# A two-block model on one core: group norms by products with a tile of ones, and the narrow rows of the recurrences made inside the delta projection

## The chip, the cores and the metric

One NeuronCore of a Trainium2 chip. The metric is the device time of the whole program in microseconds, median of three runs. Lower is better.

## The reference, cut to what matters

512 tokens of width 1024 go through a first block (band attention and a state space beside each other, attention to a memory of 256 rows, an expert layer) and twice through a hybrid layer: a gated delta rule (gdn), latent attention (mla) and a state-space duality (ssd) on the same normalised input, gated, added and projected, then a feed-forward part. The change touches normalisations of groups of channels and the small rows that steer both recurrences:

```python
def rmsnorm(x, g):
    return x * lax.rsqrt(jnp.mean(x * x, axis=-1, keepdims=True) + EPS) * g

# in the delta mixer; the duality's dt is made in the same way
beta = jax.nn.sigmoid(b_raw)
g = -jnp.exp(a_log) * jax.nn.softplus(a_raw + dt_bias)
o = gated_delta_chunked(q, k, v, g, beta)        # begins with a cumsum of g over each chunk
o = rmsnorm(o, norm_g) * jax.nn.silu(z)          # groups of 128 channels
...
mixed = g_ssd * (y_ssd @ w_ssd_out) + g_mla * (y_mla @ w_mla_out) + g_gdn * (y_gdn @ w_gdn_out)
h = x + mixed @ w_out
```

Norms that the change touches: queries and keys of the band attention (groups of 64 channels), of the attention to the memory (256), the delta rule's output (128), the duality's output (512).

## The kernel before, in words

Everything is held transposed: chunks of 128 channels on the partitions, the 512 tokens (256 for the memory) along the free side. The program is a row of stages (`stage`, L25). Within a stage each engine has its own list of instructions, ordered by semaphores; at its end the stage's semaphores are cleared one by one and all engines meet.

Projections are made by `linears` (L421). A spec `Linear` has `tiles` output tiles of 128 channels. For tile i, SP loads 512 KB of weights into one of four slots of `ring`; ACT casts them to a high part (L297), DVE subtracts that from the weights to get a low part (L307); PE makes 24 products, three for each of 8 chunks (L75 to L77); then the spec's steps run on DVE and ACT. In its turn i, ACT first casts tile i + 2, when PE has finished tile i, and DVE first makes tile i + 2's low part; then come tile i's steps, then the `norms`. Engines take their lists strictly in order. `fold` is the norm of a stage's input, made during its first two tiles (a product with a 128x128 tile of ones, L375, a root and a reciprocal of 128x512, L384). `ahead` loads the next stage's first four tiles of weights and splits two of them at the end of a stage. `behind` names the spec whose outputs are a later spec's inputs.

A `Norm` (L80) beside the tiles: ACT and DVE square half of the chunks each; PE multiplies each 128x128 block of squares with a column of ones (L126, two columns where groups are of 64), so that sums stand along partitions; ACT takes the root and DVE the reciprocal of these few columns (`roots`); PE spreads them over the partitions by products with the identity (L138), a third of the groups behind each of three tiles; DVE scales the chunks by the spread roots and a gain (L156).

Stages with such norms: mix_in (16 tiles, norm of the 8 qk chunks from tile 8), mem_in (8 wide and 16 half-width tiles, two norms), gdn_tail (gate 8, z 8, out 8, mla_in 7 tiles; norm from before tile 0), ssd_tail (gate 8, ssd_out 8, w_mix 8; norm from before tile 0, and SP refills `hT` from DRAM before the second spec's loads). The z tiles have a chain of steps: DVE evicts, ACT applies Silu, DVE multiplies, ACT casts a high part, DVE subtracts a low part (L1705 to L1717).

gdn_in makes queries, keys and values of the delta rule in 16 tiles, each with a causal convolution of four taps on DVE (L1666 to L1671) and Silu on ACT, and at last one narrow tile with the step sizes, gates and betas. Its own norm (`l2`) is not touched but for the tile it begins at. Then `narrow_rows` (L1809), a stage of its own, turns that tile into softplus, sigmoid and cumulated sums, and PE transposes them into `smallN` and `cumN` (L1820). `duality` (L1875) has the stage ssd_in and keeps its states in `ring`.

## Time and profile before

| | |
|---|---|
| median of 3 runs | 5692.46 us (5690.85 to 5692.79) |
| profiled execution, its own time | 5688.7 us |
| its span, first to last instruction | 5686.9 us |
| mean granted clock of PE | 0.932 |
| busy share of the span: PE, DVE, ACT, POOL | 91%, 52%, 29%, 12% |
| DMA, mean | 92 GB/s |

The profile lists every instruction with engine, source line, tiles, start and length, and for idle time before it what released it. A line such as L75 is that of a helper, so the same line stands for many places; the names of the tiles tell them apart. The granted clock is the share of TensorE's full speed that the chip allowed in a stretch. PEld is the loading of weights into TensorE, which overlaps its products; PEq and SPq are sequencers. The ends of PE rows are modelled.

### The profile page before, as it was taken

The numbers are of one execution on the slowest core, as the hardware profiler recorded it, in microseconds if no ns is written. First come the engines' busy times: TensorE is split into PE (matmuls) and PEld (weight loads), VectorE is DVE, ScalarE is ACT, GpSimd is POOL, SyncE is SP. The second block draws the span as 40 slices with busy tenths as digits, with TensorE's granted clock in tenths as the row PEclk, the third lists the DMA queues.
The fourth block names the chain that finished last, engine by engine and source line by source line (L and its number), as shares of the span: only waits on it lengthen the run. The fifth ranks groups of instructions, "written<-read, shape, count | busy, mean of one in ns | idle before, by whom it ended". The sixth has DMA issues, their size and how long they took to land. (4 is left out here: it accounts for less than half of the span.)

```text
span 5686.9 us, 63785 instructions
## 1 busy us (share of the span) xinstructions
PE 5165.4 (91%) x24616; PEld 4168.1 (73%) x24616; DVE 2940.1 (52%) x5436; ACT 1668.3 (29%) x2512; POOL 655.4 (12%) x412
## 2 busy tenths in 40 slices
PE   7668899999999999987899998999978999988998
PEld 6216778888878888766787675788767876767787
DVE  3584547888304444474444555444654445564433
ACT  2203433333322222232132322333321223322322
POOL 0751002222240000002200001000012100011000
PEclk9688999999999999988899998999978999989998
DMA  2002123555546555420022120222200121202222
GB/s 92 5 12 82 56 97 120 178 176 176 178 143 214 193 193 192 162 74 1 12 74 82 38 82 30 96 94 98 90 13 1 60 76 58 67 26 99 89 98 71
DMA packets 231597, 525.60 MB, mean 92 GB/s; under 512 B 19584, under 2 KB 89472, under 8 KB 230016
## 3 DMA queue, kind: packets, MB, share of 16 engines
q1 hardware_dynamic: 231296, 521.51, 27.4%
q8 instruction: 198, 3.24, 0.2%
q14 instruction: 103, 0.84, 0.0%
HBM read 445.94 MB, written 75.50 MB: 92 GB/s over the span
## 5 line engine op out<-in xcount | busy, mean ns | idle before, releaser
L307 DVE TENSOR_TENSOR weight_low<-ring,weight_high 128x1024 fp32r<-128x1024 f32 (+2 forms) x620 | 722.0, 1165 | 1502.9 <-ACT weight_high L297 1501.8
L297 ACT CAST weight_high<-ring 128x1024 fp32r<-128x1024 f32 (+2 forms) x728 | 731.8, 1006 | 2218.0 <-PE banks L77 2183.4
L75 PE MATMUL banks<-x_high,weight_high 128*128 128x512 f32 x1856 | 750.0, 404 | 104.7 <-DVE x_low L356 50.4
L76 PE MATMUL banks<-x_low,weight_high 128*128 128x512 f32 x1856 | 736.0, 397 | 0.0
L77 PE MATMUL banks<-x_high,weight_low 128*128 128x512 f32 x1856 | 734.9, 396 | 0.0
L75 PEld LDWEIGHTS banks<-x_high,weight_high 128*128 128x128 f32 x1856 | 357.5, 193 | 212.2 <-issue 100.8
L307 POOL TENSOR_TENSOR weight_low<-ring,weight_high 128x1024 fp32r<-128x1024 f32 x108 | 264.3, 2449 | 1761.8 <-ACT weight_high L297 1761.8
L77 PEld LDWEIGHTS banks<-x_high,weight_low 128*128 128x128 f32 x1856 | 356.4, 192 | 76.9
L75 PE MATMUL banks<-xn_high,weight_high 128*128 128x512 f32 x1024 | 410.7, 401 | 0.7 <-ACT hT L1390 0.7
L76 PEld LDWEIGHTS banks<-x_low,weight_high 128*128 128x128 f32 x1856 | 357.7, 193 | 72.8 <-issue 1.0
L75 PE MATMUL banks<-act_high,weight_high 128*128 128x512 f32 x1024 | 399.5, 390 | 12.7 <-DVE act_low L1597 12.7
L77 PE MATMUL banks<-xn_high,weight_low 128*128 128x512 f32 x1024 | 399.6, 390 | 0.0
L76 PE MATMUL banks<-act_low,weight_high 128*128 128x512 f32 x1024 | 399.3, 390 | 0.0
L77 PE MATMUL banks<-act_high,weight_low 128*128 128x512 f32 x1024 | 399.3, 390 | 0.0
L76 PE MATMUL banks<-xn_low,weight_high 128*128 128x512 f32 x1024 | 398.7, 389 | 0.0
L2295 POOL TENSOR_TENSOR ring<-scratch,consts_sb 128x512 f32<-128x512 f32 x96 | 122.0, 1272 | 1124.1 <-SPq L36 1005.3
L75 PEld LDWEIGHTS banks<-act_high,weight_high 128*128 128x128 f32 x1024 | 192.9, 188 | 53.2 <-issue 13.0
L77 PEld LDWEIGHTS banks<-xn_high,weight_low 128*128 128x128 f32 x1024 | 192.2, 188 | 41.3
L76 PEld LDWEIGHTS banks<-act_low,weight_high 128*128 128x128 f32 x1024 | 192.8, 188 | 40.1
L77 PEld LDWEIGHTS banks<-act_high,weight_low 128*128 128x128 f32 x1024 | 192.8, 188 | 40.1
L75 PEld LDWEIGHTS banks<-xn_high,weight_high 128*128 128x128 f32 x1024 | 192.7, 188 | 36.0 <-ACT hT L1390 0.9
L76 PEld LDWEIGHTS banks<-xn_low,weight_high 128*128 128x128 f32 x1024 | 192.8, 188 | 35.4
(580 smaller groups left out, 9327.4 us busy)
## 6 DMA issues: line engine op xcount, KB each, us to landing
ring<-in_peer_u SPq DMA_DIRECT2D x128, 512.0 KB, 3.5
ring<-in_peer_v SPq DMA_DIRECT2D x128, 512.0 KB, 3.4
acts<-dot_act SPq DMA_DIRECT2D x128, 256.0 KB, 2.0
gates<-gate_block SPq DMA_DIRECT2D x64, 512.0 KB, 6.1
activations<-acts SPq DMA_DIRECT2D x128, 256.0 KB, 3.8
gates_in<-gates SPq DMA_DIRECT2D x128, 256.0 KB, 3.9
ring<-in_w_up SPq DMA_DIRECT2D x64, 512.0 KB, 3.3
ring<-in_w_down SPq DMA_DIRECT2D x64, 512.0 KB, 3.3
```

The source lines that it names most:

```text
L75: nc.tensor.matmul(out, w_high, x_high, start=start, stop=False)
L76: nc.tensor.matmul(out, w_high, x_low, start=False, stop=False)
L77: return nc.tensor.matmul(out, w_low, x_high, start=False, stop=stop)
L297: self.nc.scalar.copy(self.wH[:, g % 2, 0:kc * P], self.ring[:, g % SLOTS, 0:kc * P]).then_inc(self.high_made, 1)
L307: ops.tensor_tensor(self.wL[:, g % 2, 0:kc * P], self.ring[:, g % SLOTS, 0:kc * P], self.wH[:, g % 2, 0:kc * P].bitcast(F32), ALU.subtract ...
L2295: nc.gpsimd.tensor_tensor(am[j % 2], AT[:, x], wide(cst("level", k * P, P)), ALU.mult).then_inc(level_ready, 1)
```

## The change

1. `GroupNorm` takes the place of `Norm` in mix_in, mem_in, gdn_tail and ssd_tail. ACT squares all chunks, DVE adds those of a group, PE multiplies once with a 128x128 tile of ones (two blocks of 64 in mix_in), which gives the sum on every partition at once; ACT takes the root of the whole 128x512 tile, DVE its reciprocal and the scalings. A group g is squared in turn at + g x pace, added one turn later, multiplied and rooted two turns later, and scaled three turns later (`at_step`). The groups begin at tiles 2 (mix_in), 3 and 11 at pace 2 (mem_in), 7 (gdn_tail) and -1 (ssd_tail).
2. In gdn_tail the 7 mla_in tiles move from the end to between gate and z.
3. A spec that is `behind` another waits for it chunk by chunk instead of for all its tiles.
4. ssd_in loads and splits the first gate weights ahead; so that `ring` is free, the duality's states are kept in scratch. The refill of `hT` in ssd_tail is issued before the third spec's loads.
5. The narrow tile becomes tile 0 of gdn_in, and `NarrowRows` makes the rows beside tiles 2 to 7; the stage `narrow_rows` is gone. The weights of both lie in one DRAM tensor.

```diff
+class GroupNorm:
...
+    def at_step(self, i, n):
+        g, rest = divmod(i - n - self.at, self.pace)
+        return [(g, range(g * self.group, (g + 1) * self.group))] if not rest and 0 <= g < self.chunks // self.group else []
+
+    def bank(self, g):
+        return self.banks[4 + g % 3][:, 0:self.n]
+
+    def act_at(self, act, i):
+        for g, chunks in self.at_step(i, 0):
+            for c in chunks:
+                if self.source:
+                    act.wait_ge(self.source.done[-1], c + 1)
+                self.nc.scalar.activation(self.scratch(c), self.x(c), ACT.Square).then_inc(self.squared, 1)
+        for g, chunks in self.at_step(i, 2):
+            act.wait_ge(self.spread, g + 1)
+            self.nc.scalar.activation(self.scratch(chunks[0]), self.bank(g), ACT.Sqrt, scale=1.0 / self.width, bias=self.eps)\
+                .then_inc(self.rooted, 1)
+        for g, chunks in self.at_step(i, 4):
+            for c in chunks if self.pair else ():
+                act.wait_ge(self.scaled, c + 1)
+                self.nc.scalar.copy(self.pair[0](c), self.y(c)).then_inc(self.high, 1)
+
+    def pe_at(self, pe, i):
+        for g, chunks in self.at_step(i, 2):
+            if self.group == 1:
+                pe.wait_ge(self.squared, g + 1)
+            else:
+                pe.wait_ge(self.added, (g + 1) * (self.group - 1))
+            if g >= 3:
+                pe.wait_ge(self.rooted, g - 2)
+            self.nc.tensor.matmul(self.bank(g), self.ones, self.scratch(chunks[0]), start=True, stop=True).then_inc(self.spread, 1)
+
+    def dve_at(self, dve, i):
+        v = self.nc.vector
+        for g, chunks in self.at_step(i, 4):
+            dve.wait_ge(self.scaled, (g + 1) * self.group)
+        for g, chunks in self.at_step(i, 1):
+            for k, c in enumerate(chunks[1:]):
+                dve.wait_ge(self.squared, c + 1)
+                if k:
+                    dve.wait_ge(self.added, g * (self.group - 1) + k)
+                v.tensor_tensor(self.scratch(chunks[0]), self.scratch(chunks[0]), self.scratch(c), ALU.add).then_inc(self.added, 1)
+        for g, chunks in self.at_step(i, 3):
+            root = self.scratch(chunks[0])
+            dve.wait_ge(self.rooted, g + 1)
+            v.reciprocal(root, root).then_inc(self.inverse, 1)
+            dve.wait_ge(self.inverse, g + 1)
+            for c in chunks:
+                v.scalar_tensor_tensor(self.y(c), self.x(c), self.gain(c), root, ALU.mult, ALU.mult).then_inc(self.scaled, 1)
+
...
-                if f == 0 and sp.behind:
-                    maker = next(x for x in specs if x.name == sp.behind)
-                    eng.wait_ge(maker.done[-1], maker.tiles)
+                maker = next((x for x in specs if x.name == sp.behind), None)
                 weights.wait_low(eng, base + i)
                 if i >= SLOTS:
                     before, b = tiles[i - SLOTS]
                     eng.wait_ge(before.bank_read, b + 1)
                 for c in range(sp.kc):
+                    if maker and f == 0:
+                        eng.wait_ge(maker.done[-1], c + 1)
...
+                    norm_qk = GroupNorm(nc, chunks_of(qkT), chunks_of(qkT), 8, 1, tools, HD1, lambda c: col("att_q_g" if c < 4 else "att_k_g"),
+                                        chunks_of(scratch), banks, 2, source=qk, ones=halves)
...
+                    norm_mq = GroupNorm(nc, chunks_of(mqT), chunks_of(mqT), 8, 2, tools, 256, lambda c: col("mem_q_g", c % 2), chunks_of(scratch),
+                                        banks, 3, 2, mq)
+                    norm_mk = GroupNorm(nc, chunks_of(mkT, n=MEM), chunks_of(mkT, n=MEM), 8, 2, tools, 256, lambda c: col("mem_k_g", c % 2),
+                                        lambda c: scratch[:, c, MEM:T], banks, 11, 2, mk)
...
+                            norm = GroupNorm(nc, chunks_of(qT), chunks_of(yT), 8, 1, tools, P, lambda c: col("gdn_g"), chunks_of(mixT), banks, 7)
                             linears(nc, "gdn_tail", [
-                                gate,
+                                gate, Linear("mla_in", dram["w_mla_in"], layer * 7, 7, DC, xn, [scaled_to(c7)]),
                                 Linear("gdn_z", dram["w_gdn_z"], layer * 8, 8, DC, xn,
                                        [scaled_to(mixT), act_in(mixT, ACT.Silu), times(yT, mixT)] + parts_of(yT, yH, yL)),
-                                out, Linear("mla_in", dram["w_mla_in"], layer * 7, 7, DC, xn, [scaled_to(c7)])], weights, banks,
-                                ahead=Ahead(weights, dram["w_mla_uq"], layer * 12, 4), norms=[norm.beside(-1)])
+                                out], weights, banks, ahead=Ahead(weights, dram["w_mla_uq"], layer * 12, 4), norms=[norm])
...
+                gate_ahead = Ahead(weights, dram["w_gate"], layer * 24)
...
+                    pre = GroupNorm(nc, chunks_of(yT), chunks_of(yT), 8, 4, tools, 512, lambda c: col("ssd_g", c), chunks_of(scratch), banks, -1,
+                                    pair=(chunks_of(yH), chunks_of(yL)))
...
+class NarrowRows:
...
+        if i != self.at + 4:
+            return
+        pe.wait_ge(self.rows_ready, 1)
+        for n, src in enumerate((self.small, self.cum)):
+            for t in range(TT):
+                s = slice(t * P, (t + 1) * P)
+                last = self.nc.tensor.transpose(self.banks[n][:, s], src[:, s], self.ident)
+            last.then_inc(self.turned, 1)
+
+    def act_at(self, act, i):
+        a = self.nc.scalar
+        if i == self.at + 1:
+            act.wait_ge(self.source.done[-1], 1)
+            a.activation(self.small[32:64, :], self.x[32:64, :], ACT.Sigmoid).then_inc(self.beta, 1)
+            act.wait_ge(self.shifted, 1)
+            a.activation(self.e, self.neg_abs, ACT.Exp).then_inc(self.magnitude, 1)
+            a.activation(self.rate, self.col("a_log"), ACT.Exp).then_inc(self.rates, 1)
+            act.wait_ge(self.magnitude, 1)
+            a.activation(self.e, self.e, ACT.Ln, bias=1.0).then_inc(self.logs, 1)
+        if i == self.at + 5:
+            for n, dst in enumerate(self.dst):
+                act.wait_ge(self.turned, n + 1)
+                a.copy(dst[:].rearrange("p a b -> p (a b)"), self.banks[n]).then_inc(self.copied, 1)
+        x, e, small, cum, ones = self.x, self.e, self.small, self.cum, self.ones
+        if i == self.at:
+            dve.wait_ge(self.source.done[-1], 1)
+            v.tensor_scalar(self.neg_abs, x, -1.0, None, ALU.mult).then_inc(self.dve_step, 1)
+            v.memset(cum[:], 0.0).then_inc(self.dve_step, 1)
+            dve.wait_ge(self.dve_step, 2)
+            v.tensor_tensor(self.neg_abs, x, self.neg_abs, ALU.min).then_inc(self.shifted, 1)
+        if i == self.at + 2:
+            dve.wait_ge(self.rates, 1)
+            dve.wait_ge(self.logs, 1)
+            dve.wait_ge(self.beta, 1)
+            v.scalar_tensor_tensor(x, x, 0.0, e, ALU.max, ALU.add).then_inc(self.dve_step, 1)
+            dve.wait_ge(self.dve_step, 3)
             v.tensor_copy(small[0:32, :], x[0:32, :])
             v.tensor_copy(small[64:128, :], x[64:128, :])
+            v.tensor_scalar(e, x, self.rate, -1.0, ALU.mult, ALU.mult).then_inc(self.dve_step, 1)
+            dve.wait_ge(self.dve_step, 4)
+        if i == self.at + 3:
+            for rows in (slice(0, 32), slice(64, 96)):
+                for t in range(TT):
+                    s = slice(t * P, (t + 1) * P)
+                    last = v.tensor_tensor_scan(cum[rows, s], ones[rows, :], e[rows, s], 0.0, ALU.mult, ALU.add)
+            last.then_inc(self.rows_ready, 1)
...
-            Linear("ssd_z", dram["w_ssd_z"], layer * 8, 8, DC, xn, z_steps)], weights, banks)
+            Linear("ssd_z", dram["w_ssd_z"], layer * 8, 8, DC, xn, z_steps)], weights, banks, ahead=ahead)
...
-        H = ring
+        H = xdd
...
-            qk = Linear("gdn_qk", dram["w_gdn_qkv"], layer * 16, 8, DC, xn,
-                        conv_steps(nc, xp, lambda f, k: col("conv_gdn", f * 4 + k), None, acc, rstd), fed=fold, lag=True)
+            qk = Linear("gdn_qk", dram["w_gdn_in"], layer * 17 + 1, 8, DC, xn,
+                        conv_steps(nc, xp, lambda f, k: col("conv_gdn", f * 4 + k), None, acc, rstd), lag=True)
             l2 = Norm(nc, lambda c: xp[:, c, 0:T], lambda c: xp[:, c, 0:T], 8, 1, tools, 1.0, None, chunks_of(squares), banks, mean=False)
+            narrow = Linear("narrow", dram["w_gdn_in"], layer * 17, 1, DC, xn, [("dve", True, narrow_scaled), ("dve", False, narrow_biased)], fed=fold)
+            rows = NarrowRows(nc, small, cum, smallN, cumN, col, ones, banks, ident, scratch, 2, narrow)
             linears(nc, "gdn_in", [
-                qk, Linear("gdn_v", dram["w_gdn_qkv"], layer * 16 + 8, 8, DC, xn,
-                           conv_steps(nc, vT, lambda f, k: col("conv_gdn", (8 + f) * 4 + k), None, acc, rstd), lag=True),
-                Linear("narrow", dram["w_narrow"], layer, 1, DC, xn, [("dve", True, narrow_scaled), ("dve", False, narrow_biased)])],
-                weights, banks, fold=fold, spill=(dram["stream"], hT[:].rearrange("p c n -> p (c n)")), norms=[l2.beside(8, source=qk)])
-        narrow_rows(nc, small, cum, smallN, cumN, col, ones, banks, ident, scratch)
+                narrow, qk, Linear("gdn_v", dram["w_gdn_in"], layer * 17 + 9, 8, DC, xn,
+                           conv_steps(nc, vT, lambda f, k: col("conv_gdn", (8 + f) * 4 + k), None, acc, rstd), lag=True)],
+                weights, banks, fold=fold, spill=(dram["stream"], hT[:].rearrange("p c n -> p (c n)")), norms=[rows, l2.beside(9, source=qk)])
```

Where this puts instructions, on the engines that wait or are waited for.

DVE in gdn_in, tiles 1 to 3 before (the last rows of a tile's convolution, the next split, the next tile):

```order
L1671 TENSOR_TENSOR gdn_qk<-banks,rstd 128x512
L1666 TENSOR_SCALAR scratch<-gdn_qk,vec 128x512
L1670 SCALAR_TENSOR_TENSOR scratch<-gdn_qk,vec,scratch 128x512 x3
L307 TENSOR_TENSOR weight_low<-ring,weight_high 128x1024
L1671 TENSOR_TENSOR gdn_qk<-banks,rstd 128x512
L1666 TENSOR_SCALAR scratch<-gdn_qk,vec 128x512
L1670 SCALAR_TENSOR_TENSOR scratch<-gdn_qk,vec,scratch 128x512 x3
L307 TENSOR_TENSOR weight_low<-ring,weight_high 128x1024
L1671 TENSOR_TENSOR gdn_qk<-banks,rstd 128x512
L1666 TENSOR_SCALAR scratch<-gdn_qk,vec 128x512
```

and in the changed kernel behind tile 2, tile 4 and tile 5 (x, neg_abs, e of `NarrowRows` are chunks of `scratch`):

```order
L1927 TENSOR_SCALAR scratch<-scratch 128x512
L1928 MEMSET cum 128x512
L1930 TENSOR_TENSOR scratch<-scratch 128x512
L379 TENSOR_TENSOR weight_low<-ring,weight_high 128x1024
...
L1746 SCALAR_TENSOR_TENSOR scratch<-gdn_qk,vec,scratch 128x512 x3
L1935 SCALAR_TENSOR_TENSOR scratch<-scratch 128x512
L1937 COPY small<-scratch 32x512
L1938 COPY small<-scratch 64x512
L1939 TENSOR_SCALAR scratch<-scratch 128x512
...
L1746 SCALAR_TENSOR_TENSOR scratch<-gdn_qk,vec,scratch 128x512 x3
L1945 SCALAR_TENSOR_TENSOR cum<-ones,scratch 32x128 x8
L379 TENSOR_TENSOR weight_low<-ring,weight_high 128x1024
```

Three pieces of rows work now stand between a tile's convolution and the next split. PE's transposes stand behind the products of tile 6:

```order
L77 MATMUL banks<-x_high,weight_low 128x512
L1904 MATMUL banks<-ident,small 128x128 x4
L1904 MATMUL banks<-ident,cum 128x128 x4
L75 MATMUL banks<-x_high,weight_high 128x512
```

So they and tile 7's products wait for the scans behind DVE's tile 5.

DVE at a z tile of gdn_tail before (`mixed` is z's room, `hT` holds y):

```order
L307 TENSOR_TENSOR weight_low<-ring,weight_high 128x1024
L1705 TENSOR_TENSOR mixed<-banks,rstd 128x512
L1712 TENSOR_TENSOR hT<-hT,mixed 128x512
L1717 TENSOR_TENSOR gdn_y_low<-hT,gdn_y_high 128x512
L307 TENSOR_TENSOR weight_low<-ring,weight_high 128x1024
```

and at the second z tile of the changed kernel, with the norm's group 6 behind it:

```order
L379 TENSOR_TENSOR weight_low<-ring,weight_high 128x1024
L1781 TENSOR_TENSOR mixed<-banks,rstd 128x512
L1788 TENSOR_TENSOR hT<-hT,mixed 128x512
L1793 TENSOR_TENSOR gdn_y_low<-hT,gdn_y_high 128x512
L291 RECIPROCAL mixed<-mixed 128x512
L294 SCALAR_TENSOR_TENSOR hT<-gdn_v,vec,mixed 128x512
L379 TENSOR_TENSOR weight_low<-ring,weight_high 128x1024
```

A reciprocal of a whole tile and a scaling follow in each of the first three z tiles. ACT at the first z tile of the changed kernel:

```order
L369 CAST weight_high<-ring 128x1024
L1785 ACT_TABLE_LOAD
L1785 ACTIVATE mixed<-mixed 128x512
L1792 CAST gdn_y_high<-hT 128x512
L261 ACT_TABLE_LOAD
L261 ACTIVATE mixed<-banks,eps 128x512
L369 CAST weight_high<-ring 128x1024
```

It loads the table of Silu (L1785) and that of the root (L261) again in each of these tiles. In the whole program the table loads become 73 from 61.

## Rows read from the trace of the kernel before

**Rows 1.** The page, part 1: busy us (share of the span), instructions.

```profile
PE 5165.4 (91%) x24616; PEld 4168.1 (73%) x24616; DVE 2940.1 (52%) x5436; ACT 1668.3 (29%) x2512; POOL 655.4 (12%) x412
```

**Rows 2.** Six stretches with norms, sums (L126) alone: us in all, busy us.

```profile
sum 231.00, PE 64.88 PEld 65.43; mean PE 10.81 PEld 10.90
```

**Rows 3.** The same six stretches, the spreads (L138) alone.

```profile
sum 231.00, PE 32.78 PEld 31.70; mean PE 5.46 PEld 5.28
```

**Rows 4.** Stretches: length, busy us (count) of each engine, granted clock, DMA share, GB/s.

```profile
94.50:102.40 7.90, 7.90 (x27) 6.05 (x27) 0.55 (x1) 0.32 (x1) 0.00 (x0) 0.70 0.00 0
2969.50:2973.00 3.50, 3.46 (x8) 2.78 (x9) 0.00 (x0) 0.00 (x0) 0.00 (x0) 0.50 0.00 0
```

**Rows 5.** Timeline, PE: start us, us, engine, line, operation, tiles, shapes, count.

```profile
29.28 0.39 PE L77 MATMUL banks<-mix_x_high,weight_low 128*128 128x512 f32 x1
29.51 1.02 PE L375 MATMUL banks<-rstd,ones 128*128 128x512 f32 x2
...
30.61 0.40 PE L76 MATMUL banks<-mix_x_low,weight_high 128*128 128x512 f32 x1
```

**Rows 6.** One line each, DVE: duration ns min/median/max, first and last start us, shapes.

```profile
L384 DVE RECIPROCAL rstd<-rstd x7: 3344/3352/3353, 32.8 to 5316.6; 128x512 f32<-128x512 f32 x7
```

**Rows 7.** The same for the scaling step of the norms.

```profile
L156 DVE SCALAR_TENSOR_TENSOR hT<-gdn_v,vec,banks x16: 737/742/745, 2894.1 to 4521.6; 128x512 f32<-128x512 f32 x16
```

**Rows 8.** Timeline of a tile of gdn_in; in brackets idle time and releaser.

```profile
4099.52 1.05 ACT L297 CAST weight_high<-ring 128x1024 fp32r<-128x1024 f32 x1 [3.86 <-PE banks L77]
...
4100.61 1.23 DVE L307 TENSOR_TENSOR weight_low<-ring,weight_high 128x1024 fp32r<-128x1024 f32 x1 [0.72 <-ACT weight_high L297]
...
4102.99 2.33 DVE L1670 SCALAR_TENSOR_TENSOR scratch<-gdn_qk,vec,scratch 128x512 f32<-128x512 f32 x3
```

**Rows 9.** Timeline of the last z tile and the first products behind it.

```profile
2963.82 1.05 ACT L297 CAST weight_high<-ring 128x1024 fp32r<-128x1024 f32 x1 [0.48 <-PE banks L77]
...
2969.54 0.79 PE L75 MATMUL banks<-gdn_y_high,weight_high 128*128 128x512 f32 x1 [5.82 <-DVE gdn_y_low L1717]
```

**Rows 10.** Timeline: first products of w_mix (layer 0).

```profile
3636.00 0.79 PE L75 MATMUL banks<-x_high,weight_high 128*128 128x512 f32 x1 [5.15 <-DVE x_low L1717]
```

**Rows 11.** Timeline: start of ssd_tail, layer 0; SPq is the DMA issue of its weights.

```profile
3521.08 5.87 SPq L290 DMA_DIRECT2D ring<-in_w_gate  x5
...
3526.65 0.79 PE L75 MATMUL banks<-x_high,weight_high 128*128 128x512 f32 x1 [8.45 <-DVE weight_low L307]
```

**Rows 12.** Timeline, first tiles of ssd_tail: a table load of ACT and what follows.

```profile
3534.93 1.28 ACT L1709 ACT_TABLE_LOAD   x1
...
3536.80 0.63 ACT L1709 ACTIVATE gdn_v<-gdn_v 128x512 f32<-128x512 f32 x1 [0.59 <-DVE gdn_v L1705]
```

**Rows 13.** Timeline, end of gdn_in to the products of the recurrence, layer 1.

```profile
4169.34 0.69 DVE L2147 TENSOR_TENSOR scratch<-banks,rstd 128x512 f32<-128x512 f32 x1 [1.80 <-PE banks L77]
...
4173.31 0.43 DVE L1839 TENSOR_SCALAR scratch<-scratch 128x512 f32<-128x512 f32 x1 [2.76 <-PEq L40]
...
4174.53 0.48 DVE L1841 MEMSET cum<- 128x512 f32 x1
...
4179.39 0.69 DVE L1846 SCALAR_TENSOR_TENSOR scratch<-scratch 128x512 f32<-128x512 f32 x1 [4.38 <-ACT scratch L1830]
...
4181.51 1.36 DVE L1853 TENSOR_TENSOR_SCAN cum<-ones,scratch 32x128 f32<-32x128 f32 x4
...
4184.30 1.12 PE L1820 MATMUL banks<-ident,small 128*128 128x128 f32 x4 [14.99 <-DVE cum L1856]
...
4188.36 1.19 PE L1863 MATMUL banks<-cum,ident 32*128 32x512 f32 x1 [2.10 <-PEq L40]
```

**Rows 14.** Timeline, early tiles of gdn_in, layer 1.

```profile
4073.86 2.33 DVE L1670 SCALAR_TENSOR_TENSOR scratch<-gdn_qk,vec,scratch 128x512 f32<-128x512 f32 x3
...
4076.11 1.22 DVE L307 TENSOR_TENSOR weight_low<-ring,weight_high 128x1024 fp32r<-128x1024 f32 x1
...
4077.38 0.50 PE L75 MATMUL banks<-x_high,weight_high 128*128 128x512 f32 x1 [2.17 <-DVE weight_low L307]
```

More of the change, by code:

```diff
@@ L469, in _ @@
             for n, sp in enumerate(specs):
-                if fill and n == 1:
-                    eng.wait_ge(norms[0].scaled, norms[0].chunks)
+                if fill and n == 2:
+                    eng.wait_ge(norms[0].low, norms[0].chunks)
                     eng.dma_start(*fill).then_inc(moved, 16)
@@ L871, in cols @@
             return vec[:, VEC1[name][0]:VEC1[name][0] + VEC1[name][1]]
-        with stage(nc, "inputs_loaded") as (block, loaded):
-            @block.sync
-            def _(sp):
-                sp.dma_start(hT[:].rearrange("p c n -> p (c n)"), dram["xT"]).then_inc(loaded, 16)
-                sp.dma_start(vec, dram["vec1"]).then_inc(loaded, 16)
-                ahead = Ahead(weights, dram["w_in"], 0)
-                ahead.sp(sp)
-                sp.wait_ge(loaded, 32)
         def norm_to(high, low, gain):
@@ L897, in mix, with _ @@
                 mixT = phase.enter_context(nc.sbuf_tensor("mixT", [P, 8, T], F32))
+                halves = mixT[:, 0, 0:P]
+                with stage(nc, "inputs_loaded") as (block, loaded):
+                    @block.sync
+                    def _(sp):
+                        sp.dma_start(hT[:].rearrange("p c n -> p (c n)"), dram["xT"]).then_inc(loaded, 16)
+                        sp.dma_start(vec, dram["vec1"]).then_inc(loaded, 16)
+                        ahead = Ahead(weights, dram["w_in"], 0)
+                        ahead.sp(sp)
+                        sp.wait_ge(loaded, 32)
+                    @block.vector
+                    def _(dve):
+                        for k in range(2):
+                            nc.vector.memset(halves[64 * k:64 * k + 64, 64 * k:64 * k + 64], 1.0)
+                            nc.vector.memset(halves[64 * k:64 * k + 64, 64 - 64 * k:128 - 64 * k], 0.0)
                 with ExitStack() as projection:
@@ L1721, in folded @@
             return Fold(nc, chunks_of(hT), DC, lambda c: col(gain, c), xn, rstd, tools, spare, banks[7])
-        def norm_to(high, low, x, gain, group=DC, width=D):
-            return Norm(nc, x, None, DC, group, tools, width, lambda c: col(gain, c), chunks_of(scratch), banks,
-                        pair=(chunks_of(high), chunks_of(low)))
         def gate_and_out(name, n, y, mixT, fed=None, home=scratch):
@@ L1847, in _ @@
             v.tensor_copy(small[0:32, :], x[0:32, :])
             v.tensor_copy(small[64:128, :], x[64:128, :])
-            link(v.tensor_scalar(e, x, rate, -1.0, ALU.mult, ALU.mult))
-            for t in range(TT):
-                s = slice(t * P, (t + 1) * P)
-                v.tensor_tensor_scan(cum[0:32, s], ones[0:32, :], e[0:32, s], 0.0, ALU.mult, ALU.add)
-            for t in range(TT):
-                s = slice(t * P, (t + 1) * P)
-                last = v.tensor_tensor_scan(cum[64:96, s], ones[64:96, :], e[64:96, s], 0.0, ALU.mult, ALU.add)
@@ L1872, in tiles4, with duality @@
     return bank.rearrange("p (t n) -> p t n", n=P)
-def duality(nc, dram, layer, xn, yT, xdt, z_steps, small, cum, smallN, cumN, col, cst, ones, ring, weights, rstd, banks, ident, scratch, acc):
+def duality(nc, dram, layer, xn, yT, xdt, ahead, z_steps, small, cum, smallN, cumN, col, cst, ones, ring, weights, rstd, banks, ident, scratch, acc):
     with ExitStack() as held:
@@ L2564, in narrow @@
         return _tiles(w)
-    d["w_narrow"] = both(narrow)
+    d["w_gdn_in"] = both(lambda l: np.concatenate([narrow(l), _tiles(part(l, 6))]))
     def mla_in(l):
```

82 lines of the change are left out of this document (31 added, 51 removed).

## The prediction

> **What bounds the kernel now.** I read the page first: PE is busy for 91% of the span and no other engine for more than 52% [rows 1]. So I looked at what PE does in the stages that the diff touches, by stretches and by its timeline. In them PE runs without a gap while a norm is made beside the tiles; the norm's small products stand in PE's own stream. That is the first thing to see: the sums against a column of ones (L126) take 64.9 us and the spreads (L138) 32.8 us in the six stretches that the diff touches (mix_in, mem_in, both layers' gdn_tail and ssd_tail) [rows 2, 3]. The second is the clock: the tile behind a block of sums runs at a granted clock of 0.70 between the levels of 1.2 and 2.4 GHz, and its 24 products take 7.9 us [rows 4]; at 0.23 us from start to start [rows 5] they would take 5.45. The third is idle PE: 5.8 us before gdn_out and 5.2 before w_mix, both until the last low part of the maker's last tile [rows 9, 10]; 8.45 before the first gate tile of ssd_tail, until a split of weights that are loaded only then [rows 11]; and 19 us around the narrow rows of the recurrence, in each layer [rows 13].
>
> **The change, part by part.** All sums are against the profiled execution, 5688.7 us (span 5686.9).
>
> *Norms.* Out go both kinds of block: 64.9 + 32.8 = 97.7, less about 3.2, since a PE row's modelled end reaches 0.16 past the next start [rows 5] and there are some 20 blocks; and six slow tiles behind them, 6 x (7.9 - 5.45) = 14.7. Together 109.2. In come 32 products of ones of full width and 4 of half width. The one that exists stands between two products that start 1.33 us apart [rows 5]; less two steps of 0.23 it costs 0.87. 32 x 0.87 + 4 x 0.44 = 29.6. PE saves **79.5**.
>
> What pays is DVE. The root is now a whole tile, so each group needs a reciprocal of 128x512 at 3.35 us [rows 6] in place of one of a few columns; the scaling stays at 0.74 [rows 7], and ACT takes over the squares that DVE made. A tile of full width already costs DVE a split of 1.2 [rows 8] and an eviction of 0.69 (the same form in [rows 13]). DVE may be late by about 3.0 before PE waits: a tile of 5.45 less cast 1.05, split 1.2 [rows 8] and two hand-overs.
> - mix_in: 1.2 + 0.69 + 3.35 + 0.74 and gaps make 6.1 a tile, against 5.45 + 0.87 = 6.3 on PE. No stall, by little.
> - mem_in: three of the four wide groups fall on half-width tiles (2.9 each, half of 5.45 and a little). Per pair DVE needs 2 x 1.6 + 0.69 + 3.35 + 2 x 0.74 = 8.7, PE 6.7: 6 us. The four narrow groups (reciprocal 1.7) are even, 6.3 against 6.3, before gaps. I take 9 in all.
> - gdn_tail: the last three groups fall on z tiles. A z tile holds DVE for 4.6: from the cast at 2963.82 to the low part that frees PE at 2969.54 are 5.7 [rows 9], its first 1.1 without DVE. With 4.1 more it is 8.7 against 6.3, 6.3 and 5.45, so 8.1 of backlog; less the 3.0, 5.2 a layer.
> - ssd_tail: two tiles carry a reciprocal and four scalings, 8.6 against 6.3 and 5.45: 5.3, less 3.0, 2.3 a layer.
>
> Together **+24**. By rows 6 a reciprocal is 3.35. The row has 3.35, and the row decides the sum.
>
> The twelve more table loads of ACT are 1.28 each [rows 12], and there the activation behind the load still waits 0.6 for DVE, so they lie in time that ACT has: nothing. The Trainium skill (ScalarE: Activation LUTs, "Step-by-step: what each stage is for") gives about 2.7 us with the drain. At that price the three z tiles that switch twice would each cost up to 2.8 more on ACT, and the sum would be some 10 us higher; rows 12 show no such drain.
>
> *Waits by chunk.* gdn_out and w_mix may begin on chunk 0 as soon as its parts are made. Seven chunks are 21 products, 4.8 us. w_mix then waits 0.4 instead of 5.15. gdn_out's last chunk comes later than now, since DVE still carries about 1.2 of the backlog: 7.0 less 4.8 leaves 2.2 of 5.8. Two layers: 2 x (4.8 + 3.6) = **-16.8**. Behind such an idle time the clock was 0.50 for 3.5 us [rows 4], 1.75 lost; of four such places I take back 1.25 each, **-5**. mla_in moves ahead of z in the same stage; its work is the same.
>
> *Gate weights ahead.* The last product before ssd_tail ends at 3518.2, the stage begins at 3521.08 [rows 11]: 5.5 of 8.45 go, and 1.3 of slow clock. At the end of ssd_in a cast and a split (1.05 + 1.2) now stand before the last tile's steps: +2.2. Two layers: **-9.2**. SP issues the same loads, four of them a stage earlier; the fill of hT waits for the last low part instead of the last scaling and stands before the load of tile 16 instead of tile 8, with some 30 us of room. POOL's list is the same.
>
> *Narrow rows.* The gap from the narrow tile's eviction at 4169.34 to 4188.36 [rows 13], 19.05, becomes the tail of a convolution tile (eviction 0.69, three taps 2.33 [rows 8, 13], and about 1.3 for the first tap, the activation and hand-overs: 4.3) plus a stage change of 2.8 [rows 13], and 0.5 for nine more semaphores to clear: 7.6. Saved 11.4 a layer. The rows are not free in the stage, though. DVE leaves tile 1 2.25 us earlier (a narrow tile has 1.2 of steps, a convolution tile 3.5), so the stall of 2.17 before tile 4 [rows 14] goes. But 1.7 of rows work (4173.31 to 4175.01) follows tile 2, 2.1 (4179.39 to 4181.51) tile 4, and 2.7 of scans tile 5 [rows 13]. Every tile has 4.7 of DVE work of its own (4100.61 to 4105.32) [rows 8] in 5.45, so nothing is caught up. ACT's chain of three loads and four activations (7 us) ends on tile 3. Walked through from 4073.9: PE waits 0.9 before tile 5 and 0.5 before tile 6; it ends tile 6 at 4092.9 and then waits in its own queue for the last scan, which DVE, 6 us behind, ends at about 4100.5. That is 7.6, with tile 7's products queued behind it; then transposes 1.9 and 1.7 of slow clock. In all 12.6 - 2.2 = 10.4. Net -1.0 a layer, **-2**. If DVE were on time the wait would still be 3.2 (1.1 + 4.7 + 2.7 against 5.45).
>
> *Clock behind the new stalls*: **+3**, an estimate from rows 4, most of them being shorter than 5 us.
>
> Sum: -79.5 + 24 - 16.8 - 5 - 9.2 - 2 + 3 = -85.5. 5688.7 - 85.5 = 5603.2; the median of the runs shown is 3.8 above the profiled execution, so **5607**.
>
> **The rivals.**
> A. *DVE hides all of it.* The squares that leave DVE and its 52% of busy time speak for it; that a reciprocal alone takes 60% of a tile speaks against. The 24 and 3 go, and the wait at tile 6 shrinks to 3.2 twice: -36, 5571.
> B. *DVE's queue is worse than walked.* Every DVE step that waits for ACT holds the queue, and in z tiles ACT itself waits for DVE twice. The stalls double (+24), the wait at tile 6 grows by 2 a layer, and the clock falls in more gaps (+4): 5639.
> C. *Slower: DVE takes over as the bound in all these stages.* Each group is then paid in full: 32 x 3.35 + 4 x 1.7 = 114, table loads 12 x 1.28 = 15, rows 2 x 10.4 = 21, together 150, against gains of 79.5 + 19.2 + 5 + 9.2 + 22.8 = 136. That is +14, 5706. It decides from where DVE has no room at all in a tile, above 5.45 without the reciprocal; now it has 1.9 in plain tiles and 4.7 in convolution tiles, without any norm in the latter.
> D. *It does nothing*: what PE no longer computes it waits for. The stretches show PE busy without a gap (7.90 of 7.90 us) [rows 4] and DVE hardly at all, so this needs the accident of equal sizes: 5692.
>
> **How the numbers follow.** Forecast 0.61, A 0.17, B 0.17, C 0.03, D 0.02. Faster and slower mean by over 0.2%, about what a measurement of this kernel can tell from no change. The forecast, A and B are faster: 0.95; D same: 0.02; C slower: 0.03. The range reaches from A, 5570, to 16 above B, 5655, for stalls and clock that add up.
>
> **What would show it.** In the profile after: L126 and L138 gone from these stages and 36 products of ones at about 0.87; seven DVE waits of 1 to 3 us before tiles 9 to 19 of mem_in and around z tiles 4 and 5 of gdn_tail; PE idle about 7.6 before the transposes inside gdn_in and about 7.6 behind its last tile; 2.2 in gdn_out, under 1 in w_mix, about 3 before the first gate tile. No idle PE in those places is rival A; waits on every tile of mix_in are C or B. A time above 5655 would mean that PE waits for DVE in tiles where I count none.

## The result, and the profile after

The changed kernel takes **5601.71 us** (median of 4 runs, 5600.65 to 5603.02) against 5691.66 beside it (5689.7 to 5692.79): ratio 0.9842, interval 0.9825 to 0.9859. The forecast was 5607. The profiled execution took 5601.1, its span is 5599.4, 87.5 below that of before.

The page of the changed kernel, part 1, against [rows 1]:

```profile
PE 5072.4 (91%) x23936; PEld 4064.4 (73%) x23936; DVE 3049.9 (54%) x5461; ACT 1714.7 (31%) x2581; POOL 655.1 (12%) x412
```

PE has 93 us less to do and DVE 110 more. The new products and reciprocals, by source line (duration ns min/median/max, first and last start us):

```profile
L276 PE MATMUL banks<-mixed,ones x32: 590/590/591, 2892.5 to 4512.2; 128*128 128x512 f32 x32
L291 DVE RECIPROCAL mixed<-mixed x16: 3342/3344/3347, 2901.9 to 4528.4; 128x512 f32<-128x512 f32 x16
```

(Each product of ones is two records here.) The reciprocal is that of [rows 6]. What pays for it is seen on PE's timeline (layer 0): two waits around the z tiles, one before the last chunk of gdn_out; then, in ssd_tail, one at its start, two beside its norm and one before the last chunk of w_mix:

```profile
2950.26 0.50 PE L75 MATMUL banks<-x_high,weight_high 128*128 128x512 f32 x1 [1.43 <-DVE weight_low L379]
2958.81 0.50 PE L75 MATMUL banks<-x_high,weight_high 128*128 128x512 f32 x1 [2.81 <-DVE weight_low L379]
2981.68 0.50 PE L75 MATMUL banks<-gdn_y_high,weight_high 128*128 128x512 f32 x1 [1.50 <-DVE gdn_y_low L1793]
...
3494.21 0.47 PE L75 MATMUL banks<-x_high,weight_high 128*128 128x512 f32 x1 [2.64 <-PEq L40]
3532.17 0.50 PE L75 MATMUL banks<-x_high,weight_high 128*128 128x512 f32 x1 [3.14 <-DVE weight_low L379]
3538.90 0.50 PE L75 MATMUL banks<-x_high,weight_high 128*128 128x512 f32 x1 [0.97 <-DVE weight_low L379]
3593.32 0.50 PE L75 MATMUL banks<-x_high,weight_high 128*128 128x512 f32 x1 [0.40 <-DVE x_low L1793]
```

The 5.82 of [rows 9] is 1.50 now (1.06 in layer 1), the 5.15 of [rows 10] is 0.40, the 8.45 of [rows 11] is 2.64. In mem_in the largest wait is not before a split but before a product of ones:

```profile
570.55 0.39 PE L75 MATMUL banks<-mem_high,weight_high 128*128 128x256 f32 x1 [1.85 <-DVE weight_low L379]
586.80 1.22 PE L276 MATMUL banks<-scratch,ones 128*128 128x256 f32 x2 [4.87 <-DVE scratch L287]
```

and on DVE what stood ahead of the addition that it waited for:

```profile
581.62 3.34 DVE L291 RECIPROCAL scratch<-scratch 128x512 f32<-128x512 f32 x1
585.00 1.41 DVE L294 SCALAR_TENSOR_TENSOR mqT<-mqT,vec,scratch 128x512 f32<-128x512 f32 x2
586.33 0.42 DVE L287 TENSOR_TENSOR scratch<-scratch 128x256 f32<-128x256 f32 x1
```

The last query group and the first key group share a tile: DVE does the one's reciprocal and scalings before the other's addition. In gdn_in of layer 1, against [rows 13]: the last scan, the transposes, and the first product of the recurrence:

```profile
4047.50 2.73 DVE L1945 TENSOR_TENSOR_SCAN cum<-ones,scratch 32x128 f32<-32x128 f32 x8
...
4050.29 1.11 PE L1904 MATMUL banks<-ident,small 128*128 128x128 f32 x4 [7.12 <-DVE cum L1945]
...
4135.61 1.19 PE L1955 MATMUL banks<-cum,ident 32*128 32x512 f32 x1 [7.72 <-PEq L40]
```

7.12 where the prediction had 7.6, and 7.72 behind the stage where it had 7.6 (7.13 and 8.02 in layer 0).

### The profile page after: what moved, and what is told of

The parts are those of the page before. It is cut to its first block and busy times, and to the rows that moved or that the text cites. A ratio compares the mean times of both kernels' runs of the same rounds, so it can differ in the third digit from the quotient of the medians.

```text
span 5599.4 us, 62522 instructions
## 1 busy us (share of the span) xinstructions
PE 5072.4 (91%) x23936; PEld 4064.4 (73%) x23936; DVE 3049.9 (54%) x5461; ACT 1714.7 (31%) x2581; POOL 655.1 (12%) x412
## 3 DMA queue, kind: packets, MB, share of 16 engines
q8 instruction: 192, 3.15, 0.2%
## 5 line engine op out<-in xcount | busy, mean ns | idle before, releaser
L1577 DVE TENSOR_SCALAR first_hot<-iota,firstT,gateT 128x128 f32<-128x128 f32 x512 | 187.6, 366 | 56.7 <-ACT gateT L1491 56.7
```

The lines of the kernel that those rows point to most:

```text
L1577: v.tensor_scalar(hotA[:, m % HOTS, k, :], iota, first[:, n:n + 1], gateT[:, n:n + 1], ALU.is_equal, ALU.mult)
```

## Experiments

Times are medians; the changed kernel is 5601.7. Stage lengths are differences of the starts of the first products of a stage and of the next one, layer 0. The stretch from latent attention to the end of ssd_in is not in the table; it took 372.3 before and 377.3 in the changed kernel, 2.3 of it the later end of ssd_in (layer 1: 372.7 and 375.0, of it 2.6).

| us | before | changed | old_norms | whole_waits | gate_late | narrow_undone |
|---|---|---|---|---|---|---|
| mix_in | 113.1 | 100.5 | 113.7 | 99.7 | 100.9 | 100.8 |
| mem_in | 119.9 | 118.5 | 125.7 | 118.6 | 119.0 | 118.5 |
| gdn_in with the rows | 139.9 | 136.7 | 136.1 | 136.7 | 136.5 | 139.6 |
| recurrence | 280.1 | 276.5 | 277.4 | 276.7 | 276.8 | 276.8 |
| gdn_tail | 201.6 | 188.4 | 196.7 | 195.9 | 189.5 | 189.5 |
| duality behind ssd_in | 95.6 | 90.7 | 90.7 | 90.6 | 97.0 | 91.1 |
| ssd_tail, to the second spec of mlp | 253.7 | 236.6 | 246.2 | 243.7 | 240.1 | 236.6 |

### The parts undone one by one

**old_norms**, in four places like this one:

```diff
-norm = GroupNorm(nc, chunks_of(qT), chunks_of(yT), 8, 1, tools, P, lambda c: col("gdn_g"), chunks_of(mixT), banks, 7)
+norm = Norm(nc, chunks_of(qT), chunks_of(yT), 8, 1, tools, P, lambda c: col("gdn_g"), chunks_of(mixT), banks)
...
-norms=[norm])
+norms=[norm.beside(-1)])
```

> The changed kernel with the old Norm (columns of ones, spreads) in mix_in, mem_in, gdn_tail and ssd_tail at its old tiles; the order of the specs, the waits by chunk, the gate weights ahead and the narrow rows stay as changed. Theory of the forecast: PE takes the 79.5 us of small products and slow tiles back, and the stalls of 24 and the 3 of clock behind them go, so +52: about 5654 against the 5601.7 of the changed kernel; no PE idle time around the z tiles of gdn_tail nor in mem_in. Rival A (DVE hides all): +80, 5681. Rival 'the gain is of the waits and the clock, the norms bring little': under +25, below 5627.

5651.6 us, +49.9. PE waits for no split around the z tiles nor in mem_in. So the norms are more than half of the gain, and rival A (+80) is out. Of mem_in's 125.7 us some 6 are not the norm's: the same instructions took 119.9 in the trace of before, and PE has no wait in either; what differs is the clock (0.88 against 0.93 over the stage).

**whole_waits**:

```diff
-                    if maker and f == 0:
-                        eng.wait_ge(maker.done[-1], c + 1)
+                    if maker and f == 0 and c == 0:
+                        eng.wait_ge(maker.done[-1], maker.tiles)
```

> The changed kernel in which the first product of a spec that is behind another waits for all of the maker's tiles again. Theory: w_mix waits 5.15 again instead of nothing, gdn_out 5.8 or more (up to 7.0) instead of 1.06, in two layers, and the clock behind these four places costs 1.25 each: +23, about 5625. In the mlp stage makers are done long before: nothing. Rival: DVE is what is late, and PE's total wait is set by it wherever PE begins: +10 or less, below 5612.

5631.0, +29.3, in the four expected places. First products of gdn_out and w_mix, and two stretches behind them (length, busy us and count of each engine, granted clock, DMA share, GB/s):

```profile
2980.00 0.76 PE L75 MATMUL banks<-gdn_y_high,weight_high 128*128 128x512 f32 x1 [6.33 <-DVE gdn_y_low L1793]
...
3601.73 0.76 PE L75 MATMUL banks<-x_high,weight_high 128*128 128x512 f32 x1 [5.24 <-DVE x_low L1793]
```

```profile
3601.73:3605.23 3.50, 3.50 (x8) 2.77 (x9) 0.00 (x0) 0.00 (x0) 0.00 (x0) 0.50 0.00 0
2980.00:2983.50 3.50, 3.50 (x8) 2.78 (x9) 0.00 (x0) 0.00 (x0) 0.00 (x0) 0.50 0.00 0
```

The wait grows by 4.8 in each of the four places, the stages by 7.5 and 6.3 (gdn_out) and 7.1 twice (w_mix): 28.1 in all, 19.3 of it waits. So 1.5 to 2.7 in each place is clock, not the 1.25 that I had taken, and the whole is 29.3 where 23 was expected.

**gate_late**:

```diff
-                gate_ahead = Ahead(weights, dram["w_gate"], layer * 24)
+                gate_ahead = None
```

> The changed kernel in which ssd_in does not load or split the first gate weights; the states stay in scratch. Theory: the wait before the first gate product becomes 8.5 from 2.64, and the end of ssd_in 2.6 from 4.8 to 5.1, so +3.5 a layer and about 1.3 of clock: +9.5 at most, 5609 to 5611. Rival: the split that moves away from the end of ssd_in takes nothing off it, as DVE is late there for other reasons: +15, 5616.

5609.4, +7.7 (four runs from 5606.3 to 5614.1, so the size is known to some 4 us; the run with the trace was 5612.2). The wait at the end of ssd_in falls back from 4.84 to 2.58, so that rival is out; the wait before the first gate product is 9.76, not 8.5, in layer 0:

```profile
3498.71 0.80 PE L75 MATMUL banks<-x_high,weight_high 128*128 128x512 f32 x1 [9.76 <-DVE weight_low L379]
```

**narrow_undone** puts the narrow spec last, drops `NarrowRows` and calls `narrow_rows` of before behind the stage.

> The changed kernel with the narrow tile last in gdn_in and the stage narrow_rows behind it, as before. Theory: gdn_in with the rows grows by the 3.2 us a layer that the traces of before and after differ by (11.3 more behind the stage, 8.1 less inside): 5608, with about 19 us between the last projection product and the first product of the recurrence. The recurrence itself was 3.7 and 2.1 us shorter in the changed kernel, by products at the higher clock. If that belongs to where the narrow rows stand, it comes back too: 5614. Rival: the rows cost in the stage all that they save behind it (0, 5602).

5609.6, but from 5602.1 to 5611.9. In its trace gdn_in is 3.0 and 2.5 longer, as expected; another 4.1 have come together by the start of mem_in, in code that is the changed kernel's. So the lowest run is as fast as the changed kernel's, and what the narrow rows gain is read from the stage, 5.5, rather than from the medians. The recurrence stays short: it does not hang on where the narrow rows stand.

The four parts add to 94.8, the whole gave 90.0. They need not add exactly, since each moves the clock of others.

### DVE's room

**recip_twice** adds in gdn_tail, ahead of each reciprocal, one more into the room that the scaling fills:

```diff
+                v.reciprocal(self.y(chunks[0]), root)
             v.reciprocal(root, root).then_inc(self.inverse, 1)
```

> The changed kernel with every reciprocal of gdn_tail made twice (the first one into the room that the scaling then fills). Theory: a plain tile has 0.3 of room left, so nearly each of 16 more reciprocals of 3.35 is paid in full, as PE waits for splits: +25 a layer, 5652, with waits before each tile of mla_in and z. Rival A (DVE has much room, or the reciprocal beside PE costs nothing): under +10.

5646.6, +44.9; gdn_tail is 25.2 and 23.6 longer. Sixteen reciprocals cost 48.8, near their 53.5 in full. In layer 0 the waits before splits (seven, 0.54 to 4.42) add to 18.2, 14 more than the 4.2 of the changed kernel; in the other 11 PE works at a lower clock:

```profile
2917.00:2980.00 63.00, 45.07 (x151) 33.58 (x152) 58.65 (x38) 18.64 (x22) 0.00 (x0) 0.85 0.14 50
```

against 1.00 in the changed kernel at 2910:2958. The clock is no second cause of these 25 us, though. The first products of the tiles start at 2917.25, 2926.24, 2935.24, 2944.23, then at 2955.99, 2967.75 and 2979.51: 9.0 apart for plain tiles and 11.8 for z tiles, however each is divided between waiting and slow work. In the plain ones DVE (the third pair of numbers) is busy for 26.87 of 26.98 us:

```profile
2917.25:2944.23 26.98, 21.44 (x78) 15.58 (x78) 26.87 (x16) 5.32 (x7) 0.00 (x0) 0.94 0.17 59
```

So DVE sets the pace. Without the added 3.3 a plain tile takes 5.7 of it where PE needs 6.35: beside its one reciprocal it has some 0.6 of room. A z tile takes 8.5 with one reciprocal and has no room for it.

**tail_norm_4**:

```diff
-... chunks_of(mixT), banks, 7)
+... chunks_of(mixT), banks, 4)
```

> The changed kernel with the norm of gdn_tail begun at tile 4 instead of 7, so that its reciprocals stand behind tiles 7 to 14 (the last gate tile and the seven mla_in tiles) and none behind a z tile. Theory: a plain tile has room for a reciprocal (6.0 of DVE in 6.3 of PE), a z tile has not; the waits of 1.43 and 2.81 before the splits around the z tiles go, in both layers, and up to 1 in gdn_out: -8.5 to -11, 5591 to 5593 against 5601.7. Rival: DVE has no room in plain tiles either and the backlog is there at the z tiles as before: under -3.

5590.1, -11.7. gdn_tail is 5.3 and 6.5 shorter, 11.8 in all, of it 8.9 of waits and 2.9 of clock. Inside the stage one wait is left, the 1.06 at gdn_out's last chunk. One reciprocal fits beside a plain tile and none beside a z tile, and gdn_out's wait is the z chain's own.

**turn_later**:

```diff
-        if i != self.at + 4:
+        if i != self.at + 6:
...
-        if i == self.at + 5:
+        if i == self.at + 7:
```

> The changed kernel with PE's transposes of the narrow rows behind tile 8 of gdn_in instead of tile 6 (and the copies of them on ACT one tile later). Theory: the 7.12 us before the transposes is DVE's backlog; PE makes two more tiles meanwhile, but tile 8 needs the split that stands behind the scans, so it waits 2.9 there. -4.2 and about 1 of clock a layer: -10, 5592. Rival: DVE catches up, all of the wait and its slow clock go: -18, 5584. Rival: the wait only moves to the split, 0, 5602.

5583.7, -18.0. This is the number of the rival, yet by the mechanism of the theory: DVE has not caught up, and PE waits 2.6 for the splits of two tiles (expected 2.9 for one):

```profile
2466.87 0.50 PE L75 MATMUL banks<-x_high,weight_high 128*128 128x512 f32 x1 [0.98 <-DVE weight_low L379]
2474.25 0.50 PE L75 MATMUL banks<-x_high,weight_high 128*128 128x512 f32 x1 [1.63 <-DVE weight_low L379]
```

gdn_in is 9.5 and 6.9 shorter, where 7.1 - 2.6 = 4.5 of wait is gone; the rest, 5.0 and 2.4, was clock. Of it 2.0 and 2.9 stood right behind the wait: the transposes take 0.79 instead of 1.62, and the 24 products behind them 5.54 instead of 6.73 and 7.56. Most of layer 0's other 3.0 lies 30 us later, at the sums of the l2 norm, which take 8.7 instead of 11.0 at a clock of 0.80 instead of 0.63 (layer 1: 10.1 and 10.2). Behind the 7.12 the changed kernel runs at 0.50, behind the 1.63 this one at 1.00:

```profile
4051.90:4055.40 3.50, 3.50 (x10) 2.79 (x9) 2.93 (x5) 0.00 (x0) 0.00 (x0) 0.50 0.43 150
```

```profile
4039.05:4043.00 3.95, 3.95 (x17) 3.28 (x18) 3.81 (x6) 0.48 (x1) 0.00 (x0) 1.00 0.40 133
```

### Two misses, and what they led to

**apart** starts mem_in's key norm at 13 instead of 11 and gives ssd_tail's norm pace 2; **apart_2** has starts 2 and 13 in mem_in and pace 3.

> The changed kernel with two norms spread out: in mem_in the key norm begins at tile 13 instead of 11, in ssd_tail the two groups go at pace 2 instead of 1. Theory: in mem_in the wait of 4.87 before the third product of ones goes (the last query group and the first key group no longer share a tile): -5; in ssd_tail one reciprocal and four scalings, 8.2 of DVE against 6.3, stay within the 3.0 by which DVE may be late, so the 3.14 and 0.97 go in both layers: -8. Together -13, 5589. Rival: DVE has no such room, stalls shift by tiles only: over -5, 5597 or more.

5604.4, no faster than the changed kernel. mem_in is 2.3 shorter (the 4.87 gone, a wait of 2.8 before a split in its place), ssd_tail 3.9 longer. The second group's additions now stand behind the first group's reciprocal and scalings, and PE's product of ones waits for them:

```profile
3514.23 1.12 PE L276 MATMUL banks<-scratch,ones 128*128 128x512 f32 x2 [0.93 <-DVE scratch L287]
...
3530.10 0.79 PE L75 MATMUL banks<-x_high,weight_high 128*128 128x512 f32 x1 [2.92 <-DVE weight_low L379]
```

> As the run that spread out two norms, but with the query norm of mem_in begun at tile 2 instead of 3, its key norm at 13, and the two groups of ssd_tail at pace 3 instead of 2. Theory: in that run the second group's three additions (2.3 us) fell behind the first group's reciprocal and four scalings in one tile, 10.5 of DVE against 6.3, and PE's product of ones waited in its queue; at pace 3 they have a tile of their own. So no wait at the first group, at most the one that goes with POOL's work on the second: ssd_tail 4 us a layer shorter than in the changed kernel. In mem_in two query groups instead of three fall on tiles of half width: 5 shorter. Together -13, 5589. Rival: any spreading costs ssd_tail, as the low parts come later than PE wants them: 5600 or more.

5606.3, a miss too. In mem_in an earlier product of ones now waits 1.7, and the stage stays at 118.7. In ssd_tail one waits 3.0 although its additions have a tile of their own; DVE comes to them late, and they take 3.15 instead of 2.27, the last with POOL beside it. Another 1.8 a layer are waits of ssd_out's products for POOL's low parts, the rival's own reason:

```profile
3525.30 1.12 PE L276 MATMUL banks<-scratch,ones 128*128 128x512 f32 x2 [3.01 <-DVE scratch L287]
```

At pace 1 all additions of ssd_tail are ahead of all reciprocals, and of the three paces tried it is the best. The rival's number held, and its reason in part.

The rows of DVE and POOL show something else, in the changed kernel:

```profile
3518.10 2.74 DVE L294 SCALAR_TENSOR_TENSOR hT<-hT,vec,scratch 128x512 f32<-128x512 f32 x4
...
3522.49 3.35 DVE L291 RECIPROCAL scratch<-scratch 128x512 f32<-128x512 f32 x1
3525.88 5.11 DVE L294 SCALAR_TENSOR_TENSOR hT<-hT,vec,scratch 128x512 f32<-128x512 f32 x4
...
3536.52 2.33 DVE L379 TENSOR_TENSOR weight_low<-ring,weight_high 128x1024 fp32r<-128x1024 f32 x1 [3.80 <-ACT weight_high L369]
```

```profile
3523.83 5.94 POOL L299 TENSOR_TENSOR ssd_y_low<-hT,ssd_y_high 128x512 fp32r<-128x512 f32 x4 [37.74 <-ACT ssd_y_high L266]
3533.97 6.03 POOL L299 TENSOR_TENSOR ssd_y_low<-hT,ssd_y_high 128x512 fp32r<-128x512 f32 x4 [4.20 <-ACT ssd_y_high L266]
```

**pool_after**:

```diff
+        if self.pair:
+            pool.wait_ge(self.scaled, self.chunks)
         for c in range(self.chunks if self.pair else 0):
             pool.wait_ge(self.high, c + 1)
```

> The changed kernel in which POOL begins the low parts of ssd_tail only when DVE has made the last of the eight scalings. In the changed kernel the second group's four scalings took 5.11 us instead of the first group's 2.74, and the split behind them 2.33 instead of 1.23, both while POOL was busy. Theory: DVE is slowed by POOL beside it; then the scalings take 2.7 again, the wait of 3.14 becomes 0.8, and one or two splits are slowed by 1.1 each instead: 1.6 to 2.4 less a layer, -4, 5598. Rival: the slow scalings have another reason (ACT, the matmuls, DMA): they stay at 5.1, 0 or worse as the low parts come later, 5602 or more.

5594.3, -7.4; ssd_tail is 3.2 shorter in both layers. The scalings are 2.74 again, the waits 0.77 and 0.27 instead of 3.14 and 0.97:

```profile
3525.89 2.74 DVE L294 SCALAR_TENSOR_TENSOR hT<-hT,vec,scratch 128x512 f32<-128x512 f32 x4
...
3534.15 1.61 DVE L381 TENSOR_TENSOR weight_low<-ring,weight_high 128x1024 fp32r<-128x1024 f32 x1 [3.79 <-ACT weight_high L371]
```

```profile
3529.82 0.50 PE L75 MATMUL banks<-x_high,weight_high 128*128 128x512 f32 x1 [0.77 <-DVE weight_low L381]
3535.82 0.50 PE L75 MATMUL banks<-x_high,weight_high 128*128 128x512 f32 x1 [0.27 <-DVE weight_low L381]
```

### The clock in the recurrence, and a faster version

> The kernel before, unchanged, for its trace alone. The recurrence was 280.1 and 279.3 us there and 276.1 to 277.9 in all others, at the same code, by products at a lower granted clock. If this clock is chance of an execution, its recurrence is 276 to 278 in at least one layer now and its time some 2 to 6 us below 5692; if it belongs to the kernel, it is 279 to 280 in both again.

One run, 5682.1, span 5680.3; its recurrence is 277.3 and 276.6. The same 80 products in a stretch of the first layer's recurrence, before, before again, changed:

```profile
2717.00:2738.00 21.00, 18.54 (x80) 13.26 (x80) 11.59 (x23) 3.35 (x6) 0.00 (x0) 0.67 0.00 0
```

```profile
2716.80:2734.80 18.00, 13.99 (x80) 10.19 (x80) 11.01 (x22) 3.34 (x6) 0.00 (x0) 0.91 0.00 0
```

```profile
2701.20:2719.20 18.00, 13.78 (x80) 9.98 (x80) 11.02 (x22) 3.35 (x6) 0.00 (x0) 0.91 0.01 1
```

The kernel before can have the short recurrence too. So the 5.7 us by which the recurrences differ between the two traces compared are taken as chance of an execution, not as the change's. How often each kernel has the long one stays open: it stands in one of two traces of the kernel before and in none of the twelve of the changed kernel and its variants (276.1 to 277.9). What makes it fall one way or the other stays open.

**combined** has tail_norm_4, turn_later and the key norm from tile 13.

> The changed kernel with the three edits that gained: the norm of gdn_tail from tile 4, the transposes of the narrow rows behind tile 8, the key norm of mem_in from tile 13. They lie in different stages, so the stages should add: -11.8 for gdn_tail, -16.4 for gdn_in, -2.3 for mem_in by the traces, 5571 against 5601.7. Rival: a tenth to a fifth is lost as the clock behind these places falls otherwise: 5576.

**5569.9** (5 runs, 5568.8 to 5571.4), ratio to before 0.9788, 0.9774 to 0.9801: faster than both kernels. Stages as in the single runs: gdn_tail 183.0, gdn_in 127.3, mem_in 115.8. Of gdn_in's gain in layer 0, 2.4 is again the clock at the l2 norm's sums (8.6 instead of 11.0). The edit of pool_after, in a stage of its own, was not run with it.

## Why the prediction was right, point by point

| term | forecast | the runs |
|---|---|---|
| PE's work for norms | -79.5 | about -76, an estimate: 50.8 by the spans of old_norms, with 24.5 of waits and some 6 of clock behind them that went with it, less the 6 of clock in its mem_in |
| waits for DVE in those stages | +24 | +24.5: mem_in 7.8, gdn_tail 4.2 twice, ssd_tail 4.1 twice |
| waits by chunk, with clock | -21.8 | -29.3, of it 19.3 of wait |
| gate weights ahead | -9.2 | -7.7 |
| narrow rows | -2 | -5.5 by stage length |
| clock behind the new stalls | +3 | about +6: 3.1 in mem_in (PE took 4.47 and 4.92 for the tiles behind the waits of 1.85 and 4.87, mostly 3.0 to 3.4 for others of half width) and the 2.9 of tail_norm_4 |
| sum | -85.5 | these terms: -88; -87.5 between the traces, -90.0 between the medians |

- **The main term and its price stand**: products of ones cost PE what the one in [rows 5] did (from one tile with one to the next is 6.35, 5.45 + 0.90), and DVE's reciprocals give some 24 back. Rivals A and D are out by this; C by its condition: DVE has room for one reciprocal in a plain tile (tail_norm_4; 5.7 of 6.35 by recip_twice). B's doubled stalls did not come.
- **Its parts were mis-sized in both directions.** "gdn_tail 5.2" was 4.2, "mem_in 9" was 7.8, and "ssd_tail 2.3" was 4.1. In mem_in I had DVE's sum per tile but only splits as what PE waits for; the product of ones has its own place in PE's queue and was the largest wait. In ssd_tail I left POOL out; pool_after shows that 3.1 of the 4.1 is POOL's doing.
- **"of four such places I take back 1.25 each" was off by most**: it was 1.5 to 2.7, 8.8 in all where 5 was taken. The row that I used shows 1.75 lost in 3.5 us, and I had taken less even than that.
- **Narrow rows**: 19.05 to 7.72 behind the stage, as forecast (11.3 against 11.4); 8.1 inside instead of 10.4: PE waited 0.47 and 0.31 before tiles 5 and 6, not 0.9 and 0.5, and 7.12, not 7.6, and the l2 norm's sums ran at a better clock (10.2 instead of 11.2 in layer 1). The "1.7 of slow clock" behind the transposes was 1.2 and 2.0 by turn_later.
- **gdn_out's last chunk**: 1.5 and 1.06 instead of 2.2. I had put 1.2 of backlog there; with no backlog (tail_norm_4) 1.06 remains.
- **Table loads at nothing** holds by the trace, though no run changes them alone: none of the 36 reciprocals has idle time of DVE before it, so none waited for ACT's root, and behind the second table load of a z tile ACT itself is idle until DVE's eviction (2.31 at 2942.28).
- **Gate weights**: "5.5 of 8.45" went, 5.8 measured; the +2.2 at the end of ssd_in was 2.3 and 2.6.

The misses partly cancel: the gains by chunk and of the narrow rows were put 11 too low, PE's work for norms 3.5 too high and the clock behind the stalls 3 too low. Part of the agreement is chance of the two traces: 5.7 of the 87.5 is the recurrence's clock, and the 2.7 by which latent attention was longer in layer 0 went the other way. The sum in the prediction has neither.

## What to carry to other kernels

When work moves from PE to another engine, add up that engine's steps tile by tile and place them where tiles have room: here three edits of numbers in the order of work were worth 32 us on top of 90. Look not only for who waits at the end of a chain, but for every small instruction in PE's queue that waits for a helper (a product of ones, a transpose), since all tiles behind it wait too. A wait of 4.9 us or more cost its length and then 1.5 to 2.9 again in clock here; one of 2 to 3 us did so in some places and not in others.

## What was not expected of the hardware

- **DVE and POOL slow each other on some forms.** Scalings whose inputs both lie in SBUF took up to 1.78 instead of 0.75 while POOL subtracted, and POOL's own went from 1.29 to 1.74 beside them and 2.28 beside a split:

```profile
L294 DVE SCALAR_TENSOR_TENSOR hT<-hT,vec,scratch x4: 740/1410/1775, 3525.9 to 3530.2; 128x512 f32<-128x512 f32 x4
L299 POOL TENSOR_TENSOR ssd_y_low<-hT,ssd_y_high x8: 1287/1303/2277, 3523.8 to 3537.7; 128x512 fp32r<-128x512 f32 x8
```

The reciprocal at 3522.49, with one input, kept its 3.35 with POOL beside it. The Trainium skill (SBUF — State Buffer, "SBUF: two separate sides") says that DVE operations with two SBUF inputs and GpSimd operations that read SBUF share a port pair under an exclusive lock, held for a whole instruction. By that rule the trace agrees: the excess, 1.0, is most of one POOL operation. The old norm's scaling read its roots from a bank, the new one reads them from SBUF. Whether the old one would have been slowed no run shows: in the kernel before, its scalings were over at 3572.0 and POOL began at 3575.27. An eviction from a bank beside POOL, at 3538.77 in the changed kernel, kept its 0.68. This rule spoke against the change and was not in the prediction: 3.2 a layer by pool_after.
- **Waits and the clock.** Behind idle times of 5.24, 6.33 and 7.12 the granted clock was 0.50 for at least 3.5 us. Behind shorter ones it fell either way. The wait of 2.81 before a z tile stands in both layers of the changed kernel, with 1.00 behind it in layer 0 and 0.55 in layer 1:

```profile
2958.81:2962.31 3.50, 3.50 (x15) 2.93 (x16) 1.93 (x3) 2.16 (x3) 0.00 (x0) 1.00 0.45 150
4533.71:4537.21 3.50, 3.50 (x9) 2.77 (x10) 1.93 (x3) 2.16 (x3) 0.00 (x0) 0.55 0.46 150
```

The 3.14 of ssd_tail had 1.00 behind it in the changed kernel and 0.50 in gate_late (layer 0 of each). So a length alone did not tell what a short wait costs.
- **The clock differs between executions of one kernel**: two traces of before have 0.67 and 0.91 for the same products, and its runs in all comparisons range from 5682.1 to 5702.1. The four of the changed kernel lie between 5600.7 and 5603.0.
